# Moving the selective scan of a hybrid decoder into its input projection, chunk by chunk

## The reference, cut to what matters

```python
z, xbc, dt = split(p)                       # SSD part of the projection
xbc = silu(causal_dwconv(xbc))              # conv of width 4 over time
xs, bm, cm = split(xbc)                     # 8 heads x 64, 2 groups x 128 state
dt = softplus(dt + dt_bias); a = -exp(a_log)
a_h = cumsum(dt * a) within each chunk of 128 tokens
decay = exp(a_h[l] - a_h[s]) for s <= l, else 0
y_diag = (cm bm^T * decay) (xs * dt)        # inside the chunk
states = bm^T (exp(a_h[end] - a_h) * xs * dt)
h_next = h * exp(a_h[end]) + states         # 8 chunks, one after the other
y = y_diag + exp(a_h) * (cm h) + xs * d_skip
y = rmsnorm_per_group(y * silu(z)) * norm_g
```

## Time and profile before

| what | value |
|---|---|
| median of 3 runs | 2736.13 us (2733.27 to 2743.95) |
| profiled execution | 2744.03 us, of which the span of its instructions 2742.3 us |
| busy in the span | PE 92%, PEld 75%, DVE 53%, ACT 36%, POOL 50% |
| mean granted clock of TensorE | 0.94 of full speed |
| DMA | 274.87 MB, 100 GB/s in the mean |

### The profile page before, as it was taken

The page is one execution under the profiler, slowest core; times in us unless marked ns, Lnnn a source line. Parts: engine busy times, 40 slices in busy tenths (PEclk is TensorE's granted clock), DMA queues, the critical chain, the costliest instruction groups (busy, mean ns, idle before and its releaser), DMA issues. The chain is left out here.

```text
span 2742.3 us, 32812 instructions
## 1 busy us (share of the span) xinstructions
PE 2535.3 (92%) x12414; PEld 2063.0 (75%) x12414; DVE 1444.6 (53%) x1476; ACT 996.6 (36%) x1581; POOL 1361.8 (50%) x802
## 2 busy tenths in 40 slices
PE   4999988998999999999979998889989999999997
PEld 3888656787788888878768875577867888887886
DVE  7553365542756555545455325645365565665543
ACT  3232344431444444333322224434234344442332
POOL 3221792422587777344312139614228777754442
PEclk7999989799999999999989998988989999999998
DMA  6612341022132232554352224301212323326442
GB/s 236 204 46 50 106 124 58 13 77 92 39 95 82 81 93 70 183 167 143 114 204 56 58 61 125 97 31 47 72 59 79 93 75 87 91 87 219 150 146 100
DMA packets 225286, 274.87 MB, mean 100 GB/s; under 512 B 32376, under 2 KB 176605, under 8 KB 223837
## 3 DMA queue, kind: packets, MB, share of 16 engines
q1 hardware_dynamic: 224829, 271.87, 31.8%
q10 hardware_dynamic: 288, 0.79, 0.1%
HBM read 227.80 MB, written 44.04 MB: 99 GB/s over the span
## 5 line engine op out<-in xcount | busy, mean ns | idle before, releaser
L768 POOL TENSOR_TENSOR wLo<-raw,wHi 128x1024 fp32r<-128x1024 f32 x60 | 166.2, 2770 | 606.5 <-ACT wHi L770 604.1
L809 POOL TENSOR_TENSOR downLo<-raw,downHi 128x1024 fp32r<-128x1024 f32 x88 | 213.3, 2426 | 280.6 <-ACT downHi L816 280.6
L1946 DVE TENSOR_TENSOR gateLo<-gateRaw,gateHi 128x512 fp32r<-128x512 f32 x88 | 204.6, 2330 | 212.7 <-ACT gateHi L1559 212.7
L1304 POOL TENSOR_TENSOR prodLo<-comb,prodHi 128x512 fp32r<-128x512 f32 x160 | 220.9, 1386 | 146.8 <-ACT prodHi L802 146.8
L1192 PE MATMUL bank<-gateHi,downHi 128*128 128x512 f32 x704 | 276.9, 393 | 14.6 <-DVE gateLo L1946 14.6
L1192 PE MATMUL bank<-gateHi,downLo 128*128 128x512 f32 x704 | 276.1, 392 | 0.0
L1192 PE MATMUL bank<-gateLo,downHi 128*128 128x512 f32 x704 | 276.0, 392 | 0.0
L828 PE MATMUL bank<-hHi,wHi 128*128 128x512 f32 x768 | 244.1, 400 | 27.7 <-DVE hLo L1668 26.3
L1176 PE MATMUL bank<-tHi,prodHi 128*128 128x512 f32 x640 | 249.7, 390 | 2.6 <-DVE part L1942 2.5
L1176 PE MATMUL bank<-tHi,prodLo 128*128 128x512 f32 x640 | 249.0, 389 | 0.0
L1176 PE MATMUL bank<-tLo,prodHi 128*128 128x512 f32 x640 | 249.0, 389 | 0.0
(11 more groups left out here) (302 smaller groups left out, 5402.7 us busy)
## 6 DMA issues: line engine op xcount, KB each, us to landing
raw<-in_ffn_w_up_dram SPq DMA_DIRECT2D x88, 512.0 KB, 4.6
raw<-in_ffn_w_down_dram SPq DMA_DIRECT2D x88, 512.0 KB, 3.8
raw<-in_ada_w_dram SPq DMA_DIRECT2D x64, 512.0 KB, 3.9
gateOut<-ua SPq DMA_DIRECT2D x44, 512.0 KB, 3.3
gateRaw<-gateOut SPq DMA_DIRECT2D x88, 256.0 KB, 2.7
raw<-in_w_in_dram SPq DMA_DIRECT2D x36, 512.0 KB, 3.8
adaE<-in_ada_w_dram SPq DMA_DIRECT2D x32, 512.0 KB, 9.0
xT<-xtail SPq DMA_DIRECT2D x8, 2048.0 KB, 9.6
```

Source lines behind the costliest of these rows:

```text
L768: eng.tensor_tensor(wLo[slot][:], raw[slot][:], fview(wHi[slot][:]), ALU.subtract).then_inc(s["split_lo"], 1)
L809: eng.tensor_tensor(dwLo[slot][:], raw[kk % 2][:], fview(dwHi[slot][:]), ALU.subtract).then_inc(s["split_lo"], 1)
L1304: pool.tensor_tensor(sLoW[idx][:], product_source(js, idx), fview(sHiW[idx][:]), ALU.subtract).then_inc(s["us_lo"], 1)
L1946: dve.tensor_tensor(dgLo[kk % 4][:], gate_slot(kk)[:], fview(dgHi[kk % 4][:]), ALU.subtract).then_inc(s["g_lo"], 1)
```

## The change

The 20 tiles get another order: MLA (3), misc, the eight `xbc` tiles (4 to 11), the four `z` tiles (12 to 15), then SWA value, key and two queries (16 to 19). The scan's stage after the attention is gone. Chunk `ch` of the scan now lies inside tile 12 + `ch`: between contraction steps of that tile PE makes the state after step 2 (chunk 7 has none), C B^T after step 4 (chunk 0: 5), and after step 6 the outputs of all eight heads and the six transposes of the next chunk. There is one set of buffers for both groups (`Mt[g]`, `Cs[g]`, one `xd`, `xe`, `bt`), so ACT's `decays(ch+1)` wait for `sd_yd` of chunk `ch`. `decays` read the cumulated rows from SBUF, where a DMA that reads one row of DRAM for all 128 rows has put them (`load_spread`); the rows are stored to DRAM once per layer.

With the order of the tiles other work moves: `dt_work` comes before the first `xbc` tile's taps on DVE; the adaLN products of DVE go, four at a time, behind the taps of the first four `xbc` tiles, and their loads come later on SP; the MLA norm is made around tiles 7 and 8; the squares of the gated output are made by POOL over all tokens after the last chunk, and PE sums them after the attention.

```diff
+T_MISC, T_XBC, T_Z, T_SV, T_SQ = 3, 4, 12, 16, 18
+SCAN0 = T_Z
...
+                def load_spread(ch):
+                    if ch:
+                        sp.wait_ge(s["sd_seg"], 2 * ch)
+                        sp.wait_ge(s["sd_eb"], 2 * ch)
+                    sp.dma_start(spreadA[:], cum_out[:, ch, :, :].to_broadcast([P, 8, BLK])).then_inc(s["cum_loaded"], 16)
...
                     if n >= AHEAD:
                         load_pack(n, kind, m)
+                    if SCAN0 + 3 <= n < N_WIN:
+                        load_spread(n - SCAN0 - 2)
...
+                def scan_turn(ch):        # PE: 6 transposes
+                    ...
+                        pe.wait_ge(s["sd_xd"], ch)
+                        pe.wait_ge(s["sd_M"], 2 * ch)
+                    for j in range(4):
+                        pe.transpose(half(2, 0)[:, j * P:(j + 1) * P], xbc[:, j, chunk_cols(ch)], ident[:])
+                    for g in range(2):
+                        last = pe.transpose(half(2, 1)[:, g * P:(g + 1) * P], xbc[:, 4 + g, chunk_cols(ch)], ident[:])
+                def scan_state(ch):
+                    ...
+                    pe.wait_ge(s["sd_xe"], ch + 1)
+                    pe.wait_ge(s["sd_bt"], ch + 1)
+                    pe.wait_ge(s["sd_h"], 1 + 2 * ch)
+                    for g in range(2):
+                        last = mm(half(3, 0)[:, g * 256:(g + 1) * 256], bt[:, g, :], xe[:, 4 * g:4 * g + 4, :], start=True, stop=True)
+                def scan_back(ch):
+                    pe.wait_ge(s["sd_M"], 2 * ch + 2)
+                    pe.wait_ge(s["sd_cs"], 2 * ch + 2)
+                    ...
+                    for h in range(SSD_HEADS):
+                        ...
+                        mm(o, xd[:, h, :], Mt[g][:, q, :], start=True, stop=False)
+                        last = mm(o, hst[ch % 2][:, h, :], Cs[g][:, q, :], start=False, stop=True)
+                    last.then_inc(s["sd_yd"], 1)
...
+                    if ch == 0:
+                        return {2: [(scan_state, 0)], 5: [(scan_scores, 0)], 6: [(scan_back, 0), (scan_turn, 1)]}
+                    return {2: [(scan_state, ch)], 4: [(scan_scores, ch)],
+                            6: [(scan_back, ch)] + ([(scan_turn, ch + 1)] if ch + 1 < NB else [])}
...
+                def scan_part(ch):        # POOL, in place of split_pre(pool, n) for n = 14 on
+                    scan_ends(ch)         # xe = xd * dte, waits sd_xd
+                    scan_decayed(ch)      # Cs[g] *= C, waits sd_eb
+                    if SCAN0 + 2 + ch < N_WIN:
+                        split_pre(pool, SCAN0 + 2 + ch)
+                    for done in ((0, 1), (2, 3), (4, 5), (6, 7))[ch - 4] if ch >= 4 else ():
+                        scan_gate(done)
...
+                    if SCAN0 + 2 <= n < N_WIN:
+                        scan_part(n - SCAN0 - 2)
+                        continue
                     if n == N_OUT0:
+                        for ch in range(N_WIN - SCAN0 - 2, NB):
+                            scan_part(ch)
+                        scan_squares()
                         ada_products()
...
+                def decays(ch):           # ACT
+                    act.wait_ge(s["cum_loaded"], 16 * (ch + 1))
+                    if ch:
+                        act.wait_ge(s["sd_yd"], ch)
+                    for g in range(2):
+                        for q in range(4):
+                            h = 4 * g + q
+                            last = A(Mt[g][:, q, :], spreadA[:, h, :], ACT.Relu, bias=adt[:, ch, h:h + 1], scale=-1.0)
+                        last.then_inc(s["sd_seg"], 1)
+                        A(Cs[g][:], spreadA[:, 4 * g:4 * g + 4, :], ACT.Exp).then_inc(s["sd_eb"], 1)
+                        act.wait_ge(s["sd_seg"], 2 * ch + g + 1)
+                        A(Mt[g][:], Mt[g][:], ACT.Exp, scale=-1.0).then_inc(s["sd_dec"], 1)
...
                 for n in range(N_WIN):
+                    if SCAN0 <= m < SCAN0 + NB - 1:
+                        decays(m - SCAN0 + 1)
                     if n + 2 < N_WIN:
                         split_pre(act, n + 2)
+                    act.wait_ge(s["pack_used"], n + 1)
...
+                    elif T_Z <= m < T_SV:
+                        A(zs[:, m - T_Z, :], ps, ACT.Silu).then_inc(free, 1)
...
                 dt_work()                 # DVE
                 for j in range(8):
                     ...                   # three taps of xbc tile j, then pair_free
+                    if j < 4:
+                        if j != 1:
+                            dve.wait_ge(s[f"ada_early_loaded{(0, 0, 1, 2)[j]}"], 16 * (8, 8, 4, 4)[j])
+                        for r in range(4 * j, 4 * j + 4):
+                            early_product(r)
...
+                for ch in range(NB):
+                    if ch:
+                        scan_turned(ch)   # xd from PSUM, bt from PSUM
+                        chunk_out(ch - 1)
+                    if ch < NB - 1:
+                        next_state(ch)
+                    for g in range(2):
+                        mix(ch, g)
+                chunk_out(NB - 1)
```

More of the change, by code:

```diff
@@ L191, in build @@
     yLo = place("ssdLo", [P, 4, T], F32R, E[8])
-    adaE = [place(f"adaE{k}", [P, D], F32, E[8 + k]) for k in range(KT)]
+    adaE = [place(f"adaE{k}", [P, D], F32, at["x"] + 4 * K * k) for k in range(KT)]
     R = [at["h"] + 4 * K * i for i in range(16)]
@@ L830, in dense_step, with dense @@
                     return last
-                def dense(pair, w_hi, w_lo, r_hi, r_lo, kts):
+                def dense(pair, w_hi, w_lo, r_hi, r_lo, kts, after={}):
                     for k in range(kts):
                         last = dense_step(pair, k, w_hi, w_lo, r_hi, r_lo, k == 0, k == kts - 1)
+                        if k < kts - 1:
+                            for part_, ch in after.get(k, ()):
+                                part_(ch)
                     return last
@@ new lines, in scan_state, with scan_scores @@
+                def scan_state(ch):
+                    if ch == NB - 1:
+                        return
+                    pe.wait_ge(s["sd_xe"], ch + 1)
[3 more added lines that the diff above has]
+                        last = mm(half(3, 0)[:, g * 256:(g + 1) * 256], bt[:, g, :], xe[:, 4 * g:4 * g + 4, :], start=True, stop=True)
+                    last.then_inc(s["sd_st"], 1)
+                def scan_scores(ch):
+                    pe.wait_ge(s["xbc_act"], 8)
+                    pe.wait_ge(s["sd_bt"], ch + 1)
+                    for g in range(2):
+                        last = mm(half(2, 1)[:, 256 + g * P:256 + (g + 1) * P], xbc[:, 4 + g, chunk_cols(ch)], xbc[:, 6 + g, chunk_cols(ch)],
+                                  start=True, stop=True)
+                    last.then_inc(s["sd_cb"], 1)
@@ L1030, in _ @@
                 pe.wait_ge(s["ml_x"], NB)
+                pe.wait_ge(s["sd_sq"], 6)
+                for g in range(2):
+                    for b in range(NB):
+                        last = mm(half(2, 1)[:, 256 + NB * g + b:257 + NB * g + b], xbc[:, 4 + 2 * g, b * P:(b + 1) * P], ones, start=True, stop=True)
+                last.then_inc(s["sd_ss"], 1)
                 for j in range(2, 6):
                     ada_sum(j)
-                pe.wait_ge(s["dt_ready"], 1)
-                pe.wait_ge(s["mod_rest"], 3)
@@ L1037, in _ @@
[L1037 to L1090, removed]
-                    mm(half(ch % 2, 1)[:, g * 256:(g + 1) * 256], bt[g][:, ch, :], xe[:, ch, 4 * g:4 * g + 4, :], start=True, stop=True).then_inc(s["sd_st"], 1)
@@ L1393, in _ @@
+                    if T_XBC <= m < T_Z:
                         j = m - T_XBC
@@ L1485, in _ @@
-                for v in range(2 * NB):
-                    ch, g = divmod(v, 2)
-                    if v in (4, 6):
-                        split_pre(act, N_OUT0 + v // 2 - 2)
-                    act.wait_ge(s["sd_bc"], v + 1)
-                    if v >= 2:
-                        act.wait_ge(s["sd_yd"], v - 1)
-                    for q in range(4):
-                        h = 4 * g + q
-                        last = A(Mt[v % 2][:, q, :], half(v % 2, 0)[:, q * P:(q + 1) * P], ACT.Relu, bias=adt[:, ch, h:h + 1], scale=-1.0)
-                    last.then_inc(s["sd_seg"], 1)
-                    A(Cs[v % 2][:], half(v % 2, 0).rearrange("p (q l) -> p q l", q=4), ACT.Exp).then_inc(s["sd_eb"], 1)
-                    act.wait_ge(s["sd_seg"], v + 1)
-                    A(Mt[v % 2][:], Mt[v % 2][:], ACT.Exp, scale=-1.0).then_inc(s["sd_dec"], 1)
-                    if g and ch >= 3:
-                        chunk_square(ch - 3)
@@ new lines, in chunk_out @@
+                def chunk_out(ch):
+                    c0 = slice(ch * BLK, (ch + 1) * BLK)
+                    dve.wait_ge(s["sd_yd"], ch + 1)
+                    for j in range(4):
+                        last = dve.scalar_tensor_tensor(out=xbc[:, j, c0], in0=xbc[:, j, c0], scalar=dcol[:, j:j + 1],
```

(24 more changed lines are left out.)

373 lines of the change are left out of this document (196 added, 177 removed).

## The result

The changed kernel takes 2752.92 us (median of 8 runs, 2748.73 to 2757.81), the kernel before on the same chip 2740.44 us (8 runs, 2733.27 to 2743.95). The ratio is 1.0051, with a 95% interval of 1.0037 to 1.0065: slower by half a per cent, 12.5 us. The forecast was 2762 us, in a range of 2726 to 2796, with slower by over 0.5% as the likeliest outcome. The profiled execution has 2751.85 us.

A forecast was written before the change was run, and what follows sets the result against it. PE was taken to bound the kernel (92% busy). Per layer -83.6 + 39.0 + 16.0 + 31.2 + 10.2 = +12.8 us, two layers +26, giving 2762 us (chance 0.43), range for 8 in 10 2726 to 2796 us.

The forecast's parts named there:

- PE's work laid in, less the norm's 5.0: In-projection: scan work added to PE, +39.0 us per layer; MLA norm's idle time and slow spreading matmuls go, 5.0.
- stall ahead of tile 6: In-projection: PE waits 13.5 us for taps behind dt's work on DVE, plus 2.5 lower clock; +16.0 us per layer.
- loop: waits at the state product: Tiles with scan chunks: PE waits for POOL's xe, queued behind a weight split that waits for ACT; +31.2 us per layer.
- clock behind those waits: After each state-product wait PE runs at the lower clock: 1.7 us for each of six chunks, +10.2 per layer.
- scan stage gone, sums left, MLA start to out-projection: After the attention: the 84.4 us scan stage goes, sums of squares of 5.8 us stay; gain 78.6 us per layer.
- the rival on the other side: Scan chunks: loop closes faster, xe ready when PE comes, waits and their clock loss go; 2679 us, chance 0.12.
- The rival that the clock holds: Scan chunks: waits cost no clock, the loop still costs 31.2 us per layer; 2741 us, no change; chance 0.2.
- the one that it falls for longer: Scan chunks: two lower-clock stretches per chunk, 20.4 us in place of 10.2, or worse; 2782 to 2800 us, chance 0.2.
- The table: ACT's decays, chunks 1 to 5: 1.28 us load at Exp on the path; rival with the page's cost 2776 us, chance 0.05.

The follow-up runs named there:

- the filler: Changed kernel plus 14 unused fp32 matmuls of 128 columns on PE ahead of the state product of chunks 1 to 6; 2735.15 us, ratio 0.9977.
- order on POOL: Changed kernel with the next chunk's xdtEnd and scaling of C moved ahead of the weight split in POOL's queue; 2667.44 us, ratio 0.9728.
- last kernel: Changed kernel plus new POOL order, early taps inside dt work, later decay-sum store and modulation reads on SP, earlier norm reciprocal on DVE; 2643.53 us, ratio 0.9666.

## Why the prediction was right

The kernels cut the time from the start of the in-projection to the MLA projections into the terms of the prediction. In us, layer 0 and layer 1: before 245.5 and 245.4; changed 332.9 and 333.1; with the filler 320.8 and 322.5; order on POOL 290.8 and 291.1; last kernel 278.1 and 279.0.

| term, per layer | predicted | measured | from |
|---|---|---|---|
| PE's work laid in, less the norm's 5.0 | +34.0 | +32.6, +33.6 | last kernel less before |
| stall ahead of tile 6, with its clock | +16.0 | +12.7, +12.1 | order on POOL less last kernel |
| loop: waits at the state product | +31.2 | +30.0, +31.4 | filler less order on POOL |
| clock behind those waits | +10.2 | +12.1, +10.6 | changed less filler |
| scan stage gone, sums left, MLA start to out-projection | -78.6 | -78.1, -81.2 | changed less before |
| sum | +12.8 | +9.3, +6.5 | |

The stretch ahead of the loop differs by up to 1.8 us between kernels that have the same code there (162.6 to 164.4 us), so single rows are good to 1 or 2 us. From the first transposes of the scan on alone, the waits are worth 31.0 and 30.9 us and the clock 10.4 and 12.0.

**The loop.** It closes where the prediction put it, for the reason it gave. PE's waits by themselves were 0.6, then 4.19 four times, 6.6 and 5.2 us, against 1.0, 4.4 four times, 6.9 and 5.7. The chunks with waits lie 20.9 to 24.3 us apart, and 18.6 us (564.3 to 582.9) are between attention and out-projection. The order on POOL, named as decisive in the rival on the other side (2679 us if the wait were gone), is decisive: 2667.44. A chunk of PE's work was 15.05 us, not 15.7, which is 5.2 us less in eight chunks. The row of the work laid in is short by only 0.4 to 1.4 us, so some 4 us of other work or lower clock in it stand in no term of the prediction; what they are was not taken apart, and that the row comes out so near is in part luck.

**The clock.** 1.7 us for each of six chunks was an estimate from one pair of rows. It held in sum, and only so: the first four chunks gave back 1.4 to 2.8 us each, the two behind gates 0.4 to 2.9. The rival that the clock holds is refuted by the filler; the one that it falls for longer (20.4 us) by the sum, and by the rows above, where it is back at full by the sixth dense row.

**The table.** Relu needs no load, so the load stands behind the four Relus and on the path, in the row at 271.61. The Trainium skill's page "ScalarE: Activation LUTs", section "Table sets: the hidden batching unit", says this of the cheap functions, and the trace agrees. The drain that its section "What ACT_TABLE_LOAD costs" adds is not seen: the activation follows 1.29 us after the load's start (271.61 to 272.90), and with the load out of four chunks the waits fell by 1.4 us each, not by the 2.66 us that the section gives for a switch.

**Where the sum was off.** The term that was mis-sized most is the stall. The step "a stall ahead of tile 6" has its wait to the tenth (13.46 against 13.5), but is worth 12.1 to 12.7 us, not 16.0 (the kernels that remove it also change the order on DVE and SP). The stretch behind it takes 82.5 us with the stall ahead of it (147.44 to 229.94) and 83.2 us without one (134.00 to 217.20): the 2.5 us of low clock don't come back. In the last kernel the one-column sums for the norms (48 records) take 9.0 us (156.0 to 165.0) and seven dense rows behind them are at the lower clock, where in the changed kernel the sums take 5.3 us (172.2 to 177.5) and four rows are. Which part of that is their place behind the stall was not tested. In layer 1 the attention piece was also 2.6 us shorter than predicted. So the trace has +15.8 us for both layers where +25.6 was predicted.

The two profiled spans differ by only +7.6 us; the other -8.2 us lie nearly all in a stage that the change doesn't touch. The down products took 251.6 and 250.8 us before and 246.2 and 247.5 after, and between 244.5 and 251.3 us in the kernels above, with the same code there, so by what the profiles show this is scatter between executions. By the medians the change costs 12.5 us, and 2752.92 lies 9 us below the forecast. The forecast stood on a median of 3 runs, 2736.13 us; on the 2740.44 us of 8 runs the same sum would have been 2766, 13 us too high. So the mechanism is right, the size of the change is about half of what was forecast, and a base that was 4 us low hides a part of that.

## What to carry to other kernels

When stages are interleaved, follow one turn through every engine's queue and look at what stands ahead of the instruction on the loop: a weight split that has 7.6 us of slack even when it goes last, issued ahead of a 1 us product that has none, cost 42 us per layer with its clock, and another order of the same instructions took them away. The same holds for the queue that issues DMAs: by the timelines a load behind a wait for something else twice ate what another edit had won, though each mending of it also moved something on DVE. Price an idle gap of a dense engine with the lower clock behind it, over a third of the wait on top here (11.2 on 31.0 us per layer).

## What was not expected of the hardware

Useless work raised the speed: 14 idle-filling matmuls in each of six waits made the kernel 0.7% faster, since the product behind them took 1.13 us instead of 2.07. And one-column matmuls brought the lower clock without idle time ahead of them. In the changed kernel the sums follow the dense rows with no wait, and the dense rows behind them are at the lower clock:

```profile
171.75 0.62 PE L852 MATMUL bank<-hHi,wLo 128*128 128x512 f32 x2
172.21 0.50 PE L985 MATMUL bank<-caus,latentSq 128*128 128x1 f32 x4
...
177.52 1.20 PE L852 MATMUL bank<-hHi,wHi 128*128 128x512 f32 x2
178.52 1.05 PE L852 MATMUL bank<-hLo,wHi 128*128 128x512 f32 x2
```

The windows view of the last kernel shows the dense rows at full clock, then 0.55 us of wait, then the norm sums with PE busy throughout and a granted clock of 0.58:

```profile
149.00:156.00 7.00, 6.46 (x29) 5.02 (x27) 6.86 (x13) 2.99 (x4) 0.00 (x0) 1.00 0.07 9
156.00:165.00 9.00, 8.99 (x48) 8.99 (x49) 8.82 (x7) 5.14 (x5) 3.05 (x1) 0.58 0.98 316
```
